# Sums of squares over heads by split squares in a two-block transformer kernel

## The reference

```
# first block, per layer: state heads (4 heads of width 128)
o = hgrn2_chunked(q_h, k_in, v_h, log_f)
o = rmsnorm(o, hgrn_norm[l]) * jax.nn.silu(hg)

# second block: queries and keys (heads of width 64, two in a tile of 128 rows)
qa = apply_rope_2(rms_norm(qa, a_q_norm_g), ang_a)      # and ka, qb, kb likewise

# second block: differential heads (4 heads of width 128)
w = p[:, :, 0] - lam * p[:, :, 1]
o = rms_norm(einsum('bhql,blhe->bqhe', w, vb), subln_g) * (1.0 - lam_init)
```

## Time and profile before

| | us |
|---|---|
| median of 3 runs | 2288.53 |
| range of the runs | 2285.6 to 2288.63 |
| the profiled execution | 2286.34 |
| its span | 2284.5 |
| TensorE busy | 2237.3 (98%) |
| VectorE busy | 1018.5 (45%) |
| ScalarE busy | 619.7 (27%) |
| GpSimd busy | 1474.6 (65%) |

### The profile page before, as it was taken

One profiled execution on the slowest core, in us unless ns is written; L12 is line 12 of the kernel. 1 busy time (PEld: TensorE's weight loads), 2 busy tenths in 40 slices (PEclk: granted clock), 3 DMA queues, 4 the chain that ended last, 5 costly groups with the idle time before them and its releaser, 6 DMA issues.

```text
span 2284.5 us, 33352 instructions
## 1 busy us (share of the span) xinstructions
PE 2237.3 (98%) x12339; PEld 1800.0 (79%) x12339; DVE 1018.5 (45%) x1563; ACT 619.7 (27%) x1103; POOL 1474.6 (65%) x1452
## 2 busy tenths in 40 slices
PE   8999999999999999999999999999999989999999
PEld 7777777888888887777788888888886567888887
DVE  6965565533331149658555333311484554333200
ACT  4333434221110024344342211110334552111100
POOL 6654765876767766549668676767483246766763
PEclk9999999999999999999999999999999999999999
DMA  5321334323333333213343332332330103233322
GB/s 187 102 74 56 107 107 152 106 93 100 93 100 93 101 109 109 69 63 103 121 139 102 102 96 97 95 98 93 123 105 11 38 1 101 93 101 92 101 92 83
DMA packets 69871, 217.53 MB, mean 95 GB/s; under 512 B 8449, under 2 KB 10753, under 8 KB 69633
## 3 DMA queue, kind: packets, MB, share of 16 engines
q1 hardware_dynamic: 54016, 188.41, 26.5%
q10 hardware_dynamic: 15744, 27.52, 3.4%
HBM read 195.93 MB, written 10.49 MB: 90 GB/s over the span
## 4 chain that ended last, share of the span: by engine, by line
PE 86%; DVE 9%; ACT 3%; issue 1%; ACTq 0%; DMA 0%; POOL 0%; DVEq 0%; POOLq 0%
PE ps L1724 77%; PE ps L2221 1%; DVE score L1504 1%; DVE xl L1601 1%; DVE small L1500 1%; DVE xl L1584 1%; DVE b_sb L1579 1%; PE ps L1990 1%; ACT pe L1067 1%; PE ps L1975 1%; PE ps L2274 1%; DVE xl L1600 1%; PE ps L2003 1%; PE ps L2241 1%; DVE small L1387 1%
## 5 line engine op out<-in xcount | busy, mean ns | idle before, releaser
L551 POOL TENSOR_TENSOR w_lo<-w_raw,w_hi 128x512 fp32r<-128x512 f32 x700 | 959.9, 1371 | 58.4
L548 POOL TENSOR_SCALAR w_hi<-w_raw 128x512 fp32r<-128x512 f32 x700 | 493.6, 705 | 623.8 <-DMA w_raw<-wst 593.1
L1724 PE MATMUL ps<-h_hi,w_lo 128*128 128x512 f32 (+1 forms) x2056 | 804.4, 391 | 10.8 <-DVE h_lo L1169 2.7
L1724 PE MATMUL ps<-h_hi,w_hi 128*128 128x512 f32 (+1 forms) x2056 | 785.2, 382 | 0.0
L1724 PE MATMUL ps<-h_lo,w_hi 128*128 128x512 f32 (+1 forms) x2056 | 785.0, 382 | 0.0
L1724 PEld LDWEIGHTS ps<-h_hi,w_lo 128*128 128x128 f32 x2056 | 387.8, 189 | 109.1 <-issue 25.1
L1724 PEld LDWEIGHTS ps<-h_lo,w_hi 128*128 128x128 f32 x2056 | 387.9, 189 | 78.0 <-issue 6.7
L1724 PEld LDWEIGHTS ps<-h_hi,w_hi 128*128 128x128 f32 x2056 | 387.7, 189 | 75.4
L1724 PE MATMUL ps<-a_hi,w_lo 128*128 128x512 f32 (+1 forms) x572 | 213.7, 374 | 0.0
L1724 PE MATMUL ps<-a_hi,w_hi 128*128 128x512 f32 (+1 forms) x572 | 213.2, 373 | 0.0
L1724 PE MATMUL ps<-a_lo,w_hi 128*128 128x512 f32 (+1 forms) x572 | 213.2, 373 | 0.0
(11 more groups left out here) (304 smaller groups left out, 2500.1 us busy)
## 6 DMA issues: line engine op xcount, KB each, us to landing
w_raw<-wst SPq DMA_DIRECT2D x350, 512.0 KB, 3.6
rot<-raw ACTq DMA_DIRECT2D x70, 128.0 KB, 3.4
gates<-gt ACTq DMA_DIRECT2D x32, 256.0 KB, 3.8
stage<-gates ACTq DMA_DIRECT2D x32, 256.0 KB, 4.1
x_sb<-xin SPq DMA_DIRECT2D x8, 256.0 KB, 5.9
out<-x_sb SPq DMA_DIRECT2D x8, 256.0 KB, 4.6
kc<-cst ACTq DMA_DIRECT2D x1, 1056.0 KB, 6.4
kc<-cst SPq DMA_DIRECT2D x1, 417.0 KB, 8.6
```

The source lines that it names most:

```text
L548: eng.tensor_scalar(w_hi[s][:, part], w_raw[s][:, part], 1.0, 1.0, ALU.mult, ALU.mult)\
L551: eng.tensor_tensor(w_lo[s][:, part], w_raw[s][:, part], w_hi[s][:, part].bitcast(F32), ALU.subtract)\
L1724: m = eng.matmul(o, w, x, start=first and i == 0, stop=final and i == 2)
```

## The change

The square of a head is split as the projections' operands are: ScalarE copies it once more into an fp32r tile (upper part), VectorE subtracts that from the square (rest, fp32r), and two fp32r matmuls against fp32r copies of the ones matrices (`ones_1`, `ones_2`, `block_2`, made by VectorE) replace the fp32 matmul. This is done for the state heads, the second block's head sums and the differential heads. The first block's query and key sums (line 1926) and the norms over the whole width stay as they are. Besides:
- the sum of state heads 0 to 2 moves from behind the cross products into the middle of the gate tile; ScalarE makes the inverse root of head h - 1 after it has evicted the cross products of head h;
- VectorE makes the rest of state head 3's square between the fourth and the fifth of the seven activation rests;
- `rope_2(r)` holds the subtract for tile r + 1 between its add and its wait for the inverse root; that for tile 0 comes ahead of all;
- in "va" the sums 11 and 12 stand behind token tiles 0 and 2, the transposes of the meta keys behind tile 1;
- for the differential heads, VectorE's subtract stands in the step with b = 1 behind the difference and ahead of the eviction.

```diff
@@ scalar: state heads
+                def head_norm(h):
+                    eng.wait_ge(oms_ready, 4 * l + h + 1)
+                    k = step(eng.activation(ors[:, :], bank(6 + h % 2), ACT.Ln, scale=1.0 / P, bias=eps))
+                    after(k)
+                    eng.activation(ors[:, :], ors[:, :], ACT.Exp, scale=-0.5).then_inc(ors_ready, 1)
...
                     eng.activation(cross[h % 2][:, :], bank(2 + 2 * (h % 2), 0, 768), ACT.Copy).then_inc(cross_taken, 1)
+                    if h:
+                        head_norm(h - 1)
...
                     eng.activation(osq[:, :], osb[:, :], ACT.Square).then_inc(osq_ready, 1)
+                    eng.wait_ge(osq_ready, 4 * l + h + 1)
+                    eng.activation(osq_hi[:, :], osq[:, :], ACT.Copy).then_inc(osq_top, 1)
                     if h == HH - 1:
                         for i in range(4, 7):
                             split_y(i)
-                    eng.wait_ge(oms_ready, 4 * l + h + 1)
-                    k = step(eng.activation(ors[:, :], bank(6 + h % 2), ACT.Ln, scale=1.0 / P, bias=eps))
-                    after(k)
-                    eng.activation(ors[:, :], ors[:, :], ACT.Exp, scale=-0.5).then_inc(ors_ready, 1)
+                head_norm(HH - 1)
@@ scalar: second block
                 eng.activation(rsq2[r % 2][:, 0:w], raw2[r % TURNS][:, 0:w], ACT.Square).then_inc(rsq_ready, 1)
+                eng.wait_ge(rsq_ready, Q0 + r + 1)
+                eng.activation(rsq_hi[r % 2][:, 0:w], rsq2[r % 2][:, 0:w], ACT.Copy).then_inc(rsq_top, 1)
...
                 eng.activation(osq2[:, :], osb2[:, :], ACT.Square).then_inc(osq2_ready, 1)
+                eng.wait_ge(osq2_ready, h + 1)
+                eng.activation(osq2_hi[:, :], osq2[:, :], ACT.Copy).then_inc(osq2_top, 1)
@@ vector
+            def square_rest(r):
+                w = 5 * META if R2_NAMES[r] == "mk" else T
+                eng.wait_ge(rsq_top, r + 1)
+                eng.tensor_tensor(rsq_lo[r % 2][:, 0:w], rsq2[r % 2][:, 0:w], rsq_hi[r % 2][:, 0:w].bitcast(F32),
+                                  ALU.subtract).then_inc(rsq_split, 1)
@@ vector, rope_2(r)
-                after(step(eng.tensor_tensor(rt3[:, 0:w], rt3[:, 0:w], rt4[:, 0:w], ALU.add)))
+                k = step(eng.tensor_tensor(rt3[:, 0:w], rt3[:, 0:w], rt4[:, 0:w], ALU.add))
+                if r + 1 < len(R2_NAMES):
+                    square_rest(r + 1)
+                after(k)
                 eng.wait_ge(rrs_ready, Q0 + r + 1)
@@ vector, state heads
                     if h == HH - 1:
-                        for i in range(7):
+                        for i in range(4):
+                            lower_y(i)
+                    eng.wait_ge(osq_top, 4 * l + h + 1)
+                    eng.tensor_tensor(osq_lo[:, :], osq[:, :], osq_hi[:, :].bitcast(F32), ALU.subtract)\
+                       .then_inc(osq_split, 1)
+                    if h == HH - 1:
+                        for i in range(4, 7):
                             lower_y(i)
@@ vector, second block
+            square_rest(0)
             for r in range(len(R2_NAMES)):
                 rope_2(r)
...
+                if b == 1 and u > PAIRS_A:
+                    eng.wait_ge(osq2_top, u - PAIRS_A)
+                    eng.tensor_tensor(osq2_lo[:, :], osq2[:, :], osq2_hi[:, :].bitcast(F32), ALU.subtract)\
+                       .then_inc(osq2_split, 1)
@@ tensor, state heads
                 def o_square(h):
-                    eng.wait_ge(osq_ready, 4 * l + h + 1)
-                    eng.matmul(bank(6 + h % 2), ones, osq[:, :], start=True, stop=True).then_inc(oms_ready, 1)
+                    eng.wait_ge(osq_top, 4 * l + h + 1)
+                    eng.wait_ge(ones_ready, l + 1)
+                    eng.matmul(bank(6 + h % 2), ones_1[:, :], osq_hi[:, :], start=True, stop=False)
+                    eng.wait_ge(osq_split, 4 * l + h + 1)
+                    eng.matmul(bank(6 + h % 2), ones_1[:, :], osq_lo[:, :], start=False, stop=True).then_inc(oms_ready, 1)
...
-                    if h:
-                        o_square(h - 1)
-                    gate_step(9 + h)
+                    name = (l, f"gate{12 + h}")
+                    c, o = half_chunk(name), begin(name)
+                    for k in range(KT):
+                        if k == KT // 2:
+                            chunk(name)
+                            if h:
+                                o_square(h - 1)
+                        m = product(o, *weights(c, k), h_hi[:, k, :], h_lo[:, k, :], k == 0, k == KT - 1)
+                    m.then_inc(w_used, 1)
@@ tensor, second block: head_sums_2 and o_square_2 alike
-                eng.matmul(bank(6 + r % 2, 0, w), block, rsq2[r % 2][:, 0:w], start=True, stop=True)\
-                   .then_inc(rms_ready, 1)
+                o = bank(6 + r % 2, 0, w)
+                eng.matmul(o, block_2[:, :], rsq_hi[r % 2][:, 0:w], start=True, stop=False)
+                eng.wait_ge(rsq_split, r + 1)
+                eng.matmul(o, block_2[:, :], rsq_lo[r % 2][:, 0:w], start=False, stop=True).then_inc(rms_ready, 1)
```

More of the change, by code:

```diff
@@ L317, in program @@
         osq2, ors2 = sbt("osq2", WK, T), sbt("ors2", WK + 2, T)
+        osq_hi, osq_lo = sbt("osq_hi", WK, T, dt=F32R), sbt("osq_lo", WK + 2, T, dt=F32R)
+        ones_1 = sbt("ones_1", WK + 4, P, dt=F32R)
+        rsq_hi = [sbt(f"rsq_hi{i}", WK + 43 + 2 * i, T, dt=F32R) for i in range(2)]
+        rsq_lo = [sbt(f"rsq_lo{i}", WK + 47 + 2 * i, T, dt=F32R) for i in range(2)]
+        block_2, ones_2 = sbt("block_2", WK + 89.5, P, dt=F32R), sbt("ones_2", WK + 8.375, P, dt=F32R)
+        osq2_hi, osq2_lo = sbt("osq2_hi", WK + 4, T, dt=F32R), sbt("osq2_lo", WK + 6, T, dt=F32R)
         posi = sbt("posi", WK, T, dt=I32)
@@ L462, in program @@
         osq2_ready = sem("osq2_ready")
+        rsq_top = sem("rsq_top")
+        rsq_split = sem("rsq_split")
+        osq_top = sem("osq_top")
+        osq_split = sem("osq_split")
+        osq2_top = sem("osq2_top")
+        osq2_split = sem("osq2_split")
+        ones_ready = sem("ones_ready")
+        sums_ready = sem("sums_ready")
         oms2_ready = sem("oms2_ready")
@@ L1648, in lower_y @@
                     eng.tensor_tensor(h_lo[:, i, :], src, h_hi[:, i, :].bitcast(F32), ALU.subtract).then_inc(ysp_lo, 1)
+                eng.tensor_copy(ones_1[:, :], ones).then_inc(ones_ready, 1)
                 for h in range(HH):
                     if h == HH - 1:
-                        for i in range(7):
+                        for i in range(4):
[5 more added lines that the diff above has]
+                        for i in range(4, 7):
                             lower_y(i)
@@ L1685, in _ @@
             eng.memset(vmz[0:2 * META, :], 0.0).then_inc(vz_clear, 1)
+            eng.tensor_copy(block_2[:, :], block).then_inc(sums_ready, 1)
+            eng.tensor_copy(ones_2[:, :], ones).then_inc(sums_ready, 1)
+            square_rest(0)
             for r in range(len(R2_NAMES)):
@@ L2146, in head_sums_2 @@
                 w = 5 * META if R2_NAMES[r] == "mk" else T
-                eng.wait_ge(rsq_ready, Q0 + r + 1)
+                eng.wait_ge(rsq_top, r + 1)
+                if r == 0:
+                    eng.wait_ge(sums_ready, 2)
                 if r >= 2:
                     eng.wait_ge(rrs_ready, Q0 + r - 1)
-                eng.matmul(bank(6 + r % 2, 0, w), block, rsq2[r % 2][:, 0:w], start=True, stop=True)\
-                   .then_inc(rms_ready, 1)
+                o = bank(6 + r % 2, 0, w)
+                eng.matmul(o, block_2[:, :], rsq_hi[r % 2][:, 0:w], start=True, stop=False)
+                eng.wait_ge(rsq_split, r + 1)
+                eng.matmul(o, block_2[:, :], rsq_lo[r % 2][:, 0:w], start=False, stop=True).then_inc(rms_ready, 1)
             for i in range(4):
@@ L2173, in _ @@
                             k == 0, k == KT - 1, True)
-                if t < 2:
-                    head_sums_2(11 + t)
-                elif t == 2:
+                if t in (0, 2):
+                    head_sums_2(11 + t // 2)
+                elif t == 1:
                     eng.wait_ge(kmt_ready, 1)
@@ L2299, in o_square_2 @@
             def o_square_2(h):
-                eng.wait_ge(osq2_ready, h + 1)
-                eng.matmul(bank(6), ones, osq2[:, :], start=True, stop=True).then_inc(oms2_ready, 1)
+                eng.wait_ge(osq2_top, h + 1)
+                eng.matmul(bank(6), ones_2[:, :], osq2_hi[:, :], start=True, stop=False)
+                eng.wait_ge(osq2_split, h + 1)
+                eng.matmul(bank(6), ones_2[:, :], osq2_lo[:, :], start=False, stop=True).then_inc(oms2_ready, 1)
             eng.wait_ge(rope_done, R0 + len(R2_NAMES))
```

## The result

The changed kernel takes 2303.91 us in the median (2301.18 to 2305.97), against 2288.58 (2285.60 to 2290.76) for the kernel before, measured beside it: the ratio is 1.0070, 95% interval 1.0058 to 1.0082, or +15.3 us. Forecast were +7.9 us and 2295.5, range 2289 to 2299. It is slower, as forecast, by nearly twice as much.

A forecast was written before the change was run, and what follows sets the result against it. TensorE, busy 98% of the span and 86% of the chain, was taken as the bound. Terms 8.4 - 2.0 + 1.5 gave +7.9 us: 2294.3 from the profiled execution, 2296.4 from the median, 2295.5 taken; range 2289 to 2299.

The forecast's parts named there:

- Price of a sum: On TensorE, two short passes cost 0.46 us against 0.86 for an fp32 sum, so each sum is 0.40 cheaper.
- Head sums: Second block: TensorE waits for VectorE's rests before sums 1 and 3; 10.7 us lost by the end of sum 5.
- S(1) to S(5): Forecast times at which VectorE has the rest of the square ready for second-block head sums 1 to 5.
- Half clock behind the long waits: TensorE after the waits before sums 1 and 3: slower tiles shorten the next wait, so nothing counted; 3.4 us the bound.
- "va", +0.6 for the late copy of the keys: Transposes move one token tile forward while ScalarE has one more conversion before their copy: 0 to 0.7 us, taken as 0.6.
- Rival 3: Half clock is not absorbed, or waits drop it more often: +3.4 us on the forecast, 2297.7 or 2299; chance 12%.
- The bound of 3.4 us for all clock effects: Limit on half-clock cost behind the two long head-sum waits, from a row where 3.8 us at lower clock cost 1.7.
- State heads: Both layers: six sums in gate tiles gain 4.4 us, the fourth sum of each layer loses 1.2; sum -2.0.
- Differential heads: ScalarE's added copy delays values: +0.65 us for three heads, -0.40 for the fourth; sum +1.5.
- rival 1: Short passes win outright, 12.0 us less, 2274.3 or 2276.5; needs 0.64 us per VectorE operation; chance 7%.
- rival 2: VectorE less held up, 0.77 us an operation: second-block stage 0, kernel -0.5, 2285.8 or 2288.0; chance 15%.
- The forecast's own bounds of +3.5 and +9.6: Whole kernel: +3.5 us if VectorE's added subtract takes 0.69, up to about +9.6; 2290 to 2298.

The follow-up runs named there:

- e11_keys_early: Whole change, but ScalarE copies the meta keys one step earlier, ahead of the last head's norm: 2295.39 us against 2287.85 for the kernel before, +7.5.
- e4_va_old: Whole change, but sums 11 and 12 and the meta keys' transposes in the old order: 2295.85 us against 2287.55 for the kernel before, +8.3.
- e1_state: Kernel before with only the state heads' part of the change: 2284.43 us against 2287.33, ratio 0.9986.
- e3_diff: Kernel before with only the differential heads' part of the change: 2288.53 us, ratio 1.0008.
- e5_no_rest: Whole change without the rests of the head sums' squares, the second pass rereading the upper part (norm incorrect): 2290.35 us, +3.0 over the kernel before.
- e2_heads: Kernel before with only the second block's short head sums and their new order in "va": 2302.56 us, ratio 1.0067, +15.2.
- e13_best: Kernel before plus short sums for state heads 0 to 2 and head sums 6 to 10, rests first in rope_2: 2281.88 us against 2287.85, -6.0.

## Why the prediction was wrong, by its steps

The direction and most terms of the sum held; the step that failed is the one for "va", below.

- **Price of a sum, 0.40.** Right: in the whole change, from sum 5 to sum 10 the delay falls from 10.8 to 8.9, 1.9 for five sums.
- **Head sums, +10.7 up to sum 5.** Right, with 10.1 measured. VectorE's five operations a head alternate as priced, but for the last head, which takes 6.2 us and not 7.1. Its rests end at 1650.3, 1656.8, 1663.9, 1670.3 and 1676.5, against S(1) to S(5) of 1649.8, 1656.25, 1663.4, 1669.8 and 1676.9. The two waits show as 4.40 and 4.03 us plus slow passes, where the prediction wanted 4 to 5 and over 6; the second is shorter because the half clock behind the first makes qb1 end at 1659.0 and not at 1655.7: the time is spent in the tile. Three rows of VectorE:

```profile
1648.59 1.75 DVE L1373 TENSOR_TENSOR rsq_lo<-rsq,rsq_hi 128x512 fp32r<-128x512 f32 x1
...
1655.68 1.10 DVE L1373 TENSOR_TENSOR rsq_lo<-rsq,rsq_hi 128x512 fp32r<-128x512 f32 x1
...
1662.10 1.75 DVE L1373 TENSOR_TENSOR rsq_lo<-rsq,rsq_hi 128x512 fp32r<-128x512 f32 x1
```

- **Half clock behind the long waits, counted at nothing.** Right behind the first: TensorE runs at half clock in the 5.6 us behind it, and VectorE still sets the time of sum 3. Behind the second it came out otherwise. Tile qb2 takes 1.0 us longer than at full clock (its first pass starts at 1664.50, sum 4 at 1671.02, 6.5 us instead of 5.5), and sums 4 and 5 find their rests ready and don't wait. The slow tile stands in for the waits of 0.5 and 1.2 us that the forecast had there; that the two come to nearly the same is luck.

```profile
1650.40:1656.00 5.60, 5.60 (x13) 4.44 (x14) 5.45 (x5) 3.06 (x5) 5.43 (x5) 0.50 0.13 47
```

- **"va", +0.6 for the late copy of the keys.** This is the step that failed. The wait came, and at 0.46 us it is the size forecast; what it sets off was not in the sum. Rival 3 allowed the waits to drop the clock more often, but priced that with the two long waits, at 3.4 us. The 13.6 us at half clock cost 6.8 (an estimate, half their length), with the wait 7.3; by the medians, the whole change less e11_keys_early is 7.8. Without that the change costs +8.3 (e4_va_old) or +7.5 (e11_keys_early), against +7.9 forecast. The bound of 3.4 us for all clock effects, taken from the one stretch of the earlier trace rows, made the range too narrow: it treats the time at half clock as given by one row. Each of the other terms came within 0.6 us of its forecast.
- **State heads, -2.0.** Right. The projection passes behind the cross products of head 0 start 2.94 us later than in the kernel before, those behind the fourth sum 1.78; in the second layer 1.82 and 0.72. That is a gain of 1.2 and 1.1, 2.3 in all; e1_state gives 2.9, with an interval from 1.1 to 5.3. The fourth sum waits 0.99 us and costs 1.0 more, forecast 1.2.
- **Differential heads, +1.5.** Right. A unit is 0.68 longer, forecast 0.65, and the values wait 0.72 us for the late eviction in each of the three units; e3_diff alone +1.2 with an interval around zero.
- **Rivals 1 and 2** fall with the rows of VectorE. VectorE's five operations take some 6.5 us a head, 1.3 each, where rival 1 needed 0.64 and rival 2 0.77. e5_no_rest shows besides that the short passes gain less than the 12 us of rival 1 even with the rest left out: its +3.0 less the 7.8 of "va" is -4.8, in part because ScalarE's conversion makes TensorE wait 2.3 us before sum 3.
- **The arithmetic.** 2286.34 + 7.9 is 2294.2, not 2294.3. The forecast's own bounds of +3.5 and +9.6 don't follow from its terms: 4.7 - 2.0 + 1.5 is 4.2, and 9.7 - 2.0 + 1.5 is 9.2. Neither matters for the miss.

## What to carry to other kernels

Before a split operand replaces an fp32 one, find where two uses stand with no other work between them: there the maker of the split sets the time, and the fp32 pair is the cheaper one (all short head sums lost 15 us, about half of it by the clock in "va"; with those of heads 6 to 10 alone nothing waited there). A new wait of half a microsecond is not priced by its length: look at the granted clock behind it, and if an earlier copy on another engine takes the wait away, take it away. Measure equal passes by their spacing before believing a busy share.

## What was not expected of the hardware

The granted clock fell from 1.00 to 0.50 behind a wait of 0.46 us and stayed there for 13.6 us with TensorE never idle, in passes of 128 columns; in e2_heads it was 10.2 us, in e5_no_rest 13.6. The long waits, 3.3 us and 4.0 to 4.6 us in the head sums, brought 3.4 to 6.8 us at half clock; behind the 2.30 us in e5_no_rest the clock stayed. None of the traces shows why the clock returned as late as it did in "va". The Trainium skill, page "TensorE: Matmul & The Clock Gate", section "A second HAM failure mode: psum-queue depth-cycling", tells of a kernel in which TensorE idles shortly and often between groups of matmuls, and the clock swings between its two levels. No trace here shows that: in "va" a single wait stands ahead of the fall.

Whether the clock falls behind a given wait also differs from trace to trace. In all thirteen, TensorE waits 1.9 to 2.0 us for VectorE at the same place, near 1613; behind it the clock is 0.50 for 3.4 us in four (the kernel before, the whole change, e1_state, e13_best) and stays at 1.00 in nine. What decides that isn't shown. Near 140 us, from 280 to 290 and from 1075 to 1090, too, stretches of 3.4 us at half clock (6.8 in the kernel before, at 1075) stand in some of the thirteen traces and not in others, in places that no edit touches; each 3.4 us is worth 1.7, half its length, which is part of the spread between executions.
